# A hybrid decoder step on one core: unscaled feed-forward inputs, the norm's root applied in PSUM, a grouped last tile and a GpSimd copy

## The reference

```python
def rmsnorm(x, w):
    xf = x.astype(jnp.float32)
    y = xf * lax.rsqrt(jnp.mean(xf * xf, axis=-1, keepdims=True) + EPS)
    return (y * w.astype(jnp.float32)).astype(x.dtype)

def swiglu(h, wg, wu, wd):
    return (jax.nn.silu(h @ wg) * (h @ wu)) @ wd

# for each layer
x = x + mixer(rmsnorm(x, norm_mix_w[i]))
x = x + swiglu(rmsnorm(x, norm_ffn_w[i]), ffn_w_gate[i], ffn_w_up[i], ffn_w_down[i])
# at the end
y = rmsnorm(x, norm_final_w)
```

## Time and profile before

| | |
|---|---|
| median of three runs | 3465.35 us |
| the profiled execution | 3463.11 us |
| its span, first to last instruction | 3461.2 us |
| mean granted TensorE clock | 0.975 |
| busy: TensorE, VectorE, GpSimd, ScalarE | 3209.8, 1663.6, 1208.0, 782.7 us |
| GpSimd w_hi and w_lo, 230 each | 452.4 and 605.7 us |

### The profile page before, as it was taken

One profiled execution on the slowest core, in us unless ns is written; L12 is line 12 of the kernel. 1 busy time (PEld: TensorE's weight loads), 2 busy tenths in 40 slices (PEclk: granted clock), 3 DMA queues, 4 the chain that ended last, 5 costly groups with the idle time before them and its releaser, 6 DMA issues.

```text
span 3461.2 us, 47065 instructions
## 1 busy us (share of the span) xinstructions
PE 3209.8 (93%) x20050; PEld 3074.6 (89%) x20050; DVE 1663.6 (48%) x1899; ACT 782.7 (23%) x1115; POOL 1208.0 (35%) x528
## 2 busy tenths in 40 slices
PE   6999888988789999999987999999987999999997
PEld 5898788888779999999977897988976999999997
DVE  6343656565552222222386858768686322232224
ACT  4212324224240000000044414233144100000002
POOL 2222302112024343343333545446462343433432
PEclk9999999999999999999999999999998999999998
DMA  4111101001011111111112213122130111111111
GB/s 142 68 50 62 41 25 38 32 29 40 14 36 43 49 49 43 49 43 49 43 40 77 95 55 116 50 94 83 61 119 31 47 43 49 45 48 49 43 49 62
DMA packets 79236, 190.76 MB, mean 55 GB/s; under 512 B 20900, under 2 KB 36932, under 8 KB 78920
## 3 DMA queue, kind: packets, MB, share of 16 engines
q1 hardware_dynamic: 52384, 150.03, 12.9%
q10 hardware_dynamic: 26664, 37.88, 3.4%
HBM read 164.07 MB, written 19.59 MB: 53 GB/s over the span
## 4 chain that ended last, share of the span: by engine, by line
PE 78%; DVE 12%; issue 4%; ACT 3%; POOL 1%; DMA 1%; ACTq 0%; DVEq 0%; SPq 0%; POOLq 0%
PE ps_set L551 64%; PE ps_core L823 4%; PE ps_set L560 2%; PE ps_core L1015 2%; ACT work L1079 1%; DVE work L1802 1%; DVE work L1594 1%; DVE work L1918 1%; PE ps_core L1020 1%; ACT L1079 1%; DVE work L2129 1%; DMA w_raw<-in_w 1%; PE ps_set L635 1%; DVE work L2144 1%; DVE conv_s L1805 1%
## 5 line engine op out<-in xcount | busy, mean ns | idle before, releaser
L475 POOL TENSOR_TENSOR w_hi<-w_raw,small 128x1024 fp32r<-128x1024 f32 x230 | 452.4, 1967 | 2079.5 <-PE ps_set L551 1848.4
L551 PE MATMUL ps_set<-h_hi,w_hi 128*128 128x344 f32 x3696 | 809.6, 327 | 18.2 <-ACT work L1079 14.9
L551 PE MATMUL ps_set<-h_lo,w_hi 128*128 128x344 f32 x3696 | 784.8, 321 | 0.0
L551 PE MATMUL ps_set<-h_hi,w_lo 128*128 128x344 f32 x3696 | 780.8, 320 | 0.0
L551 PEld LDWEIGHTS ps_set<-h_hi,w_hi 128*128 128x128 f32 x3696 | 621.5, 189 | 38.9 <-issue 20.6
L551 PEld LDWEIGHTS ps_set<-h_lo,w_hi 128*128 128x128 f32 x3696 | 625.8, 189 | 0.0
L551 PEld LDWEIGHTS ps_set<-h_hi,w_lo 128*128 128x128 f32 x3696 | 616.3, 188 | 0.0
L478 POOL TENSOR_TENSOR w_lo<-w_raw,w_hi 128x1024 fp32r<-128x1024 f32 x230 | 605.7, 2634 | 18.1
L2016 DVE TENSOR_TENSOR work<-work,ps_set 128x1032 f32<-128x1032 f32 x44 | 54.1, 1229 | 786.8 <-PE ps_set L551 776.9
L1669 DVE TENSOR_TENSOR x<-x,ps_set 128x1032 f32<-128x1032 f32 x160 | 196.7, 1229 | 256.4 <-PE ps_set L551 256.4
L551 PE MATMUL ps_set<-y_hi,w_hi 128*128 128x344 f32 x1296 | 285.1, 329 | 15.8 <-ACT work L1079 7.5
(11 more groups left out here) (219 smaller groups left out, 3519.4 us busy)
## 6 DMA issues: line engine op xcount, KB each, us to landing
w_raw<-in_w SPq DMA_DIRECT2D x230, 512.0 KB, 3.3
work<-ssm_cum_rows ACTq DMA_DIRECT2D x32, 512.0 KB, 4.3
sample<-in_ssm_state SPq DMA_DIRECT2D x16, 512.0 KB, 4.2
out_ssm_s<-sample SPq DMA_DIRECT2D x16, 512.0 KB, 2.6
x<-in_x SPq DMA_DIRECT2D x6, 688.0 KB, 15.2
work<-work ACTq DMA_DIRECT2D x16, 258.0 KB, 2.4
out_y<-x SPq DMA_DIRECT2D x6, 688.0 KB, 3.4
sample<-bc_rows SPq DMA_DIRECT2D x8, 512.0 KB, 4.9
```

The lines of the kernel that those rows point to most:

```text
L475: return nc.gpsimd.tensor_tensor(w_hi[:, k, :], w_raw[:, k, :], zeros, ALU.add)
L551: mm = nc.tensor.matmul(out[:, g, 0:TN], w[:, slot, cols], v[:, g * TN:(g + 1) * TN], start=(start and n == 0), stop=(stop and n == 2))
```

## The change

In both feed-forwards the input halves no longer hold the norm's root. At boundaries 1 and 3 ScalarE makes `h_hi` directly as x times weight, and VectorE makes `h_lo` as x times weight minus `h_hi`. Neither needs the root, so TensorE goes on to the first two tiles after all outputs, and the mean squares stand between their groups. The root is made once, for all 1032 tokens, with one exponential. Gate is multiplied by it out of PSUM before silu; silu's result is multiplied by it again before it meets up. The second half of each pair is then multiplied, rounded and subtracted by token group. The last up tile of each feed-forward is made group after group, and the last down products wait for their own group alone. On GpSimd the high part is written by a copy, without the zeros and without the wait for the constants, and its loops are unrolled; ScalarE's and VectorE's last loop turn is peeled.

```diff
-            zeros = ZERO.to_broadcast([P, 1024])
-            pool.wait_ge(consts_in, 48)
-
             def high(k):
-                return nc.gpsimd.tensor_tensor(w_hi[:, k, :], w_raw[:, k, :], zeros, ALU.add)
+                return nc.gpsimd.tensor_copy(w_hi[:, k, :], w_raw[:, k, :])
...
-            with pool.Fori(1, SSM0 // 2) as i:
-                split(i, 0)
-                split(i, 1)
+            for unit in range(2, SSM0):
+                split(0, unit)
...
@@ TensorE, boundary
+                if n in (1, 3):
+                    for g in range(TG):
+                        outputs_of(g)
+                    projections(0)
+                    mean_square(0)
+                    projections(1)
+                    mean_square(1)
+                    projections(2, lambda: mean_square(2))
+                    return
...
@@ TensorE, feed-forward
+                def by_group(jobs, job, turn, unit):
+                    part = take(jobs, job, turn)
+                    pe.wait_ge(w_split, unit + 1)
+                    for g in range(TG):
+                        for c in range(KC):
+                            mm = group_products(ps_set[part][:, g, :], unit % 2, c, (h_hi[:, c, :], h_lo[:, c, :]), g,
+                                                c == 0, c == KC - 1)
+                        mm.then_inc(*((unit_done, 1) if g == TG - 1 else (part_done, 1)))
...
+                pe.wait_ge(*ffn_dve[m].value(f"loB{g}", PAIRS - 1))
                 for q in range(4):
                     if g == 0 and q % 2 == 0:
-                        pe.wait_ge(*ffn_dve[m].value("loB", PAIRS - 1))
                         pe.wait_ge(w_split, unit + q // 2 + 1)
...
@@ ScalarE, boundary
+                def products(g):
+                    for c in range(KC):
+                        if c % 2 == 0:
+                            act.wait_ge(*x_pair_ready(n, g, c // 2))
+                        fn(h_hi[:, c, span(g)], x[:, c, span(g)], ACT.Identity, scale=NORM_W[:, n, c:c + 1])\
+                            .then_inc(*norm_act[n].step(f"hi{c}.{g}"))
...
+                if n in (1, 3):
+                    products(0)
+                    squares(0)
+                    products(1)
+                    products(2)
+                    squares(1)
+                    squares(2)
+                    if n == 3:
+                        act.wait_ge(prompt_out[2], 16 * GROUPS)
+                    for g in range(TG):
+                        logs(g)
+                    for g in range(TG):
+                        act.wait_ge(*core.read(f"ms{g}"))
+                    fn(RSTD, RSTD, ACT.Exp, scale=-0.5).then_inc(*norm_act[n].step("rstd"))
+                    return
...
@@ ScalarE, feed-forward
+                def silu(jobs, gate, turn, c):
+                    act.wait_ge(*jobs.read(gate, turn))
+                    fn(tok(c), tok(c), ACT.Silu).then_inc(*ffn_act[m].step("silu" + "AB"[c]))
...
@@ VectorE, boundary
+                def lows(g, first, last):
+                    for c in range(first, last):
+                        dve.wait_ge(*norm_act[n].value(f"hi{c}.{g}"))
+                        v.scalar_tensor_tensor(h_lo[:, c, span(g)], x[:, c, span(g)], NORM_W[:, n, c:c + 1],
+                                               h_hi[:, c, span(g)].bitcast(F32), ALU.mult, ALU.subtract)\
+                            .then_inc(*norm_dve[n].step(f"lo{c}.{g}"))
...
+                if n == 1:
+                    add(0, 0)
+                    for g in range(TG):
+                        for q in range(1, 4):
+                            add(g, q)
+                            lows(g, 2 * q - 2, 2 * q)
+                        if g + 1 < TG:
+                            add(g + 1, 0)
+                        lows(g, 6, 8)
+                        if g == 1:
+                            sums(0)
+                    sums(1)
+                    sums(2)
+                    return
+                if n == 3:
+                    for g in range(TG):
+                        lows(g, 0, 4)
+                        if g == TG - 1:
+                            sums(0)
+                        for q in (2, 3):
+                            add(g, q)
+                            lows(g, 2 * q, 2 * q + 2)
+                    sums(1)
+                    sums(2)
+                    return
...
@@ VectorE, feed-forward
+                def gate(jobs, name, turn, unit, c, pair, before):
+                    dve.wait_ge(unit_done, unit + 1)
...
+                    v.tensor_tensor(grp(tok(c)), grp(RSTD), big(jobs.part(name)), ALU.mult).then_inc(jobs.sem(name), 1)
+                    dve.wait_ge(*ffn_act[m].value("silu" + "AB"[c], pair))
+                    v.tensor_tensor(tok(c), tok(c), RSTD, ALU.mult).then_inc(*ffn_dve[m].step("f" + "AB"[c]))
...
+                def gated_b(jobs, up, turn, unit, pair, last=False):
...
+                    own("fB", pair)
+                    for g in range(TG):
+                        if last and g < TG - 1:
+                            dve.wait_ge(part_done, parts + (PAIRS - 1) * 6 + g + 1)
+                        else:
+                            dve.wait_ge(unit_done, unit + 1)
+                        v.tensor_tensor(tok(3)[:, span(g)], tok(1)[:, span(g)], ps_set[jobs.part(up)][:, g, 0:TN], ALU.mult)\
+                            .then_inc(*((jobs.sem(up), 1) if g == TG - 1 else ffn_dve[m].step(f"gB{g}")))
+                        if g:
+                            low(g - 1)
+                    low(TG - 1)
```

More of the change, by code:

```diff
@@ L58 @@
 FFN0_PARTS = GDN_PARTS + (HEADS - 1) * (KC - 1) + (4 * TG - 1)
[L59 removed]
+FFN_PARTS = (PAIRS - 1) * 2 * 3 + (TG - 1) + (4 * TG - 2)
 SSM_PARTS = FFN0_PARTS + FFN_PARTS
@@ L527, in _ @@
                 split(0, unit)
-            with pool.Fori(FFN1 // 2, UNITS // 2) as i:
-                split(i, 0)
-                split(i, 1)
+            for unit in range(FFN1, UNITS):
+                split(0, unit)
         @block.tensor
@@ L2010, in ffn @@
                 first, loop = (big_jobs[f"ffn{m}{s}"] for s in ("a", ""))
-                def gated(jobs, gate, up, turn, unit, c):
+                own = lambda name, turn=0: dve.wait_ge(*ffn_dve[m].value(name, turn))
+                def gate(jobs, name, turn, unit, c, pair, before):
                     dve.wait_ge(unit_done, unit + 1)
-                    dve.wait_ge(*jobs.read(gate, turn))
-                    v.tensor_tensor(grp(tok(2 + c)), grp(tok(c)), big(jobs.part(up)), ALU.mult).then_inc(jobs.sem(up), 1)
@@ L2018, in low @@
-                def low(c, pair):
-                    dve.wait_ge(*ffn_act[m].value("hi" + "AB"[c], pair))
-                    v.tensor_tensor(y_lo[:, c, :], tok(2 + c), y_hi[:, c, :].bitcast(F32), ALU.subtract)\
-                        .then_inc(*ffn_dve[m].step("lo" + "AB"[c]))
-                gated(first, "ga", "ua", 0, base + 1, 0)
-                low(0, 0)
-                gated(first, "gb", "ub", 0, base + 3, 1)
-                low(1, 0)
-                with dve.Fori(0, (PAIRS - 1) // 2) as i:
-                    for k in range(2):
-                        unit = i * 12 + (base + 4 + 6 * k)
-                        gated(loop, f"ga.{k}", f"ua.{k}", i, unit + 1, 0)
-                        add_outputs(loop, [f"out{t}.{k}" for t in range(KC)], i, unit + 2, i * 12 + (parts + 6 * k))
-                        low(0, i * 2 + (k + 1))
-                        gated(loop, f"gb.{k}", f"ub.{k}", i, unit + 5, 1)
-                        low(1, i * 2 + (k + 1))
+                    if before is None:
+                        dve.wait_ge(*norm_act[2 * m + 1].value("rstd"))
+                    else:
+                        own(("loA", f"loB{TG - 1}")[c], before)
@@ new lines, in pair @@
+                def pair(i, k, last=False):
+                    unit = i * 12 + (base + 4 + 6 * k)
+                    count = i * 2 + (k + 1)
+                    gate(loop, f"ga.{k}", i, unit, 0, count, i * 2 + k)
+                    gated_a(loop, f"ua.{k}", i, unit + 1, count)
+                    add_outputs(loop, [f"out{t}.{k}" for t in range(KC)], i, unit + 2, i * 12 + (parts + 6 * k))
+                    low_a(count)
+                    gate(loop, f"gb.{k}", i, unit + 4, 1, count, i * 2 + k)
+                    gated_b(loop, f"ub.{k}", i, unit + 5, count, last)
@@ L2037, in front_tile @@
+                gate(first, "ga", 0, base, 0, 0, None)
+                gated_a(first, "ua", 0, base + 1, 0)
+                low_a(0)
+                gate(first, "gb", 0, base + 2, 1, 0, None)
+                gated_b(first, "ub", 0, base + 3, 0)
+                with dve.Fori(0, (PAIRS - 1) // 2 - 1) as i:
+                    pair(i, 0)
+                    pair(i, 1)
+                pair((PAIRS - 1) // 2 - 1, 0)
+                pair((PAIRS - 1) // 2 - 1, 1, True)
             def front_tile(k, gr):
```

84 lines of the change are left out of this document (54 added, 30 removed).

## The result

The changed kernel takes 3410.89 us (median of 4 runs, 3408.81 to 3412.83), against 3465.68 (3461.84 to 3466.24) for the kernel before on the same chip: ratio 0.9844, 95% interval 0.9827 to 0.9861. The profiled execution has a span of 3411.0 us.

What follows compares the result with a forecast made beforehand. TensorE was taken as the bound, with time to win only at feed-forward ends, boundaries and GpSimd waits. Terms -13, -7.4, -3.3, +2.5 and 0 took 3463.1 to 3441.9, about 3444 with 2.2 added; stated 3443 us, range 3427 to 3458.

Steps and rivals of the forecast that it cites:

- What bounds the kernel: Whole kernel: TensorE busy 3209.8 of 3461.2 us; only feed-forward ends, boundaries and waits for GpSimd can pay.
- Last tile by group: Ends of both feed-forwards: down products' pair 0.2 starts 6.5 us sooner each, -13 us together (-8 to -16.6).
- GpSimd copy: GpSimd's w_hi operations: each takes 1.0 us instead of 1.97, few splits hold anyone, -7.4 us (+3 to -14).
- Boundary 1: Before the first feed-forward: no wait for the root, but a longer VectorE line, -3.3 us (-6 to +1).
- Boundary 3: Before the second feed-forward: VectorE's line takes turns with GpSimd and delays the projections, +2.5 us.
- Loop: Gate and up in the feed-forward loop: 106 us more VectorE work, hidden with 5.8 us spare, 0 us.
- Sum: Whole kernel: -13 - 7.4 - 3.3 + 2.5, given as -21 us.
- (a): Rival, boundaries give all they can: boundary 1 -6, boundary 3 -9; 3429 us, 3424 with larger copy gains; chance 0.18.
- (b): Rival, GpSimd's copy costs as much as the addition; about 3453 to 3456 us; chance 0.15.
- (c): Rival, in the feed-forward loop the second product ends too late, delaying first outputs in 44 halves; 3487 us; chance 0.04.

Runs made afterwards that it cites:

- the loops alone: The kernel before with only GpSimd's two splitting loops written out, w_hi still adding zeros: 3464.67 us, ratio 1.0003.
- 27 tiny memsets: The changed kernel with 27 GpSimd memsets of one w_lo column ahead of each w_hi copy: 3437.50 us, ratio 0.9924.
- one long memset: The changed kernel with one GpSimd memset of the whole w_lo slot ahead of each w_hi copy: 3429.80 us, ratio 0.9909.
- the second copy: The changed kernel with one more GpSimd copy of w_raw, into w_lo's slot, ahead of each w_hi: 3453.97 us, ratio 0.9971.
- quarters of w_lo: The changed kernel with each w_lo subtraction issued as four operations of 256 elements: 3406.93 us, ratio 0.9834.

## Why the prediction was wrong

**What bounds the kernel.** Right in outline: bodies unchanged, gains in ends, boundaries and waits for GpSimd. The last of these I looked for in the wrong place: in TensorE's waits, and not in VectorE's stretched operations.

**Last tile by group, -13.** Right in mechanism and near in size: undoing the part costs 13.5 us by the medians and about 11 at the two ends by the shifts. The order of turns that I worked out is what the trace shows (TensorE's pause before pair 0.2 is 1.3 us, 1.8 forecast).

**GpSimd copy, -7.4 (to -14).** This is the step that failed. Its mechanism was right and its price per operation too (1.0 against 1.04 us); the number of places was off, and with it the term, which should have been -37. The prediction named eight places (boundaries 0 and 2, four group ends, two like collisions). In the kernel before, 59 VectorE operations outside the bodies are stretched under a w_hi, by 63 us in all. "Nearly all splits are hidden" was read off TensorE's waits for w_lo. But a VectorE operation that is held by GpSimd's turn shows as VectorE busy, not as anyone's wait: TensorE's row then names VectorE. In stages where VectorE's line is the path, the evidence was in the lengths of its operations, and I had used just that for the feed-forward ends, three operations of some 0.55 us in 5.27 and four tiny ones in 2.93, without asking how many such rows the serial stages hold. The upper end, -14, should have been worked out from there: the stretched operations under w_hi put the most that the copy could give near 63 us.

The Trainium skill's rule from SBUF — State Buffer, Who interferes with whom, that a VectorE instruction with two SBUF inputs and a GpSimd instruction reading SBUF exclude each other for a whole instruction, was cited against this change. The trace agrees with it in both directions (3.42 us for 1.23, and 4.26 for 1.04), and here it worked mostly for the change. Of the estimate that I made from the Trainium skill, GPSIMD Engine Reference, Elementwise — side-by-side cycle accounting, 0.9 to 1.5 us for the copy, the lower end was the nearer one: it takes 1.04.

**Boundary 1, -3.3.** Measured 6.9, of which the copy alone 0.5. Everything in front of it had moved by 9.0, so the forecast start of the projections, 971.3, stands for 962.3; they began at 961.2. From there to the end of the third mean square I had 26.5 us and it took 23.9; from that to the body I had 4.4 and it took 4.4 (985.1 to 989.55). (My four terms for it add up to 4.1 only.) The over-priced term is the mean squares, at 2.3 each. On the chain of waits of the changed kernel each takes 1.16; the 2.65 of the earlier trace rows, from which I priced them, stands at the end of the kernel and holds the wait for their result. That is 3.4 us for the three, and the up tile was not 0.6 late; some 1.4 us went the other way, since the projections began at half clock (0.50 granted from 961.2 to 964), which I had left out.

```profile
970.33 1.16 PE ps_core L574 x4
```

**Boundary 3, +2.5.** Measured -1.1, so the term was off by 3.6. The copy's own part is -3.0 against the kernel before (-4.2 against the loops alone); the rest of the change costs it 1.9 us (shift -43.5 less -33.9 behind it, -42.4 less -30.9 ahead). The pause of some 10 us before the projections came as 3.4 among the outputs and 6.6 before the projections. So the cause was right, VectorE's line in turns with GpSimd, and the sign came out only for the rest of the change, without the copy.

**Loop, 0.** Right: 704.6 us for the first body and the shift unchanged (-43.5) over the second; the second product takes 2.26 us on average, inside the 5.8 spare.

**Sum.** Copy -37, ends -12 (14.9 us in the table, less 2.4 of the copy's), boundary 1 -6, boundary 3 +2: -53, with -54.8 timed and -50.2 in the traces. Had the copy's term been -37, the prediction's sum would have been 3414.

**Rivals.** (a) came nearest in time, with 3429 or 3424, but for another reason: boundary 1 did give its 6, boundary 3 gave 1 and not 9, and the rest came from the copy in the serial stages, where it had allowed 5 us for "larger copy gains". (b), a copy as dear as the addition, and (c) did not happen.

**Still open.** Whether 27 tiny memsets really cost more than one long memset, whose trace has the same length; how the 43 us of the second copy divide exactly between delay and reading; and why quarters of w_lo, which shorten VectorE's serial operations by as much as the copy did, gain so little even with TensorE's 5.7 us of waits counted in.

## What to carry to other kernels

When two engines exclude each other at a memory, their waits hide in busy time: compare each operation's length in the serial stages with its undisturbed length, and count how many are stretched, before pricing an edit that shortens the other engine's turn. That count tells roughly the most that can be won and not the price, since only what stands on the path reaches the end. Here an operation off the critical path, 0.83 us shorter in each of 230 turns, moved the end by 37 us, as if 45 of them had stood on it. Cutting such turns in pieces gave 7 us at most, and each further piece has a fixed cost of some 0.2 us.

## What the runs showed of the hardware

- GpSimd's copy of 128x1024 fp32 into fp32r takes 1.04 us undisturbed, the addition of a broadcast column 1.9, a subtraction of two full operands 2.40 (512 elements: 1.30, 256: 0.74), a memset 0.95, and a memset of one column 0.10, of which nine are through in 0.31.
- The hold between VectorE and GpSimd goes both ways: a VectorE operation of 1.23 us took 3.42, and a GpSimd copy of 1.04 took 4.26.
- Not only VectorE operations with two SBUF inputs are held. In the kernel before, copies of 8 elements with one input, 0.16 us alone, take up to 2.37 us; here VectorE, then GpSimd:

```profile
2043.62 2.37 DVE L1805 COPY conv_s<-work 128x8 f32<-128x8 f32 x1
...
2043.23 2.73 POOL L478 TENSOR_TENSOR w_lo<-w_raw,w_hi 128x1024 fp32r<-128x1024 f32 x1
```

- VectorE operations that read PSUM are not held (242 beside GpSimd, none over 0.01 us too long), and a GpSimd memset, which reads nothing, hardly holds any (4 of 47; a copy in its place 38 of 75).
- A delay of 0.9 us on an engine that TensorE did not wait for cost 19 to 27 us by the medians, 15 to 16 by the traces. TensorE's new waits for the split are 5.4 to 5.9 us of it; that the rest comes from shifting GpSimd's reads against VectorE's is what the counts above suggest, and not shown apart.
